# Modulation sums moved from GpSimd and ScalarE to VectorE, norm roots applied behind the products, and a reordered start

## The reference, cut to what matters

```python
for l in range(2):
    h = rms_norm(x, attn_norm[l])
    if l == 0: x = x + diff_attention(h, ...)           # 8 heads
    else:
        kw, vw = shared_kv(x, cos, sin, kv_norm, w_kv, k_norm)
        x = x + swa_sink_attention(h, ..., kw, vw)
    x = x + swiglu(rms_norm(x, ffn_norm[l]), w_gate_up[l], w_down[l])   # (silu(g) * u) @ w_down
```

```python
m = silu(cond) @ w_mod + b_mod      # cond: c and c_ctx; w_mod: 1024 x 6144, for two layers
h = rmsnorm(x, norm) * (1 + scale) + shift
```

## Time and profile before

| | |
|---|---|
| median of 3 runs | 3081.02 us (3073.94 to 3084.14) |
| profiled execution | 3078.21 us |
| its span, first to last instruction | 3076.3 us |
| mean granted TensorE clock | 0.953 |
| busy: TensorE, VectorE, ScalarE, GpSimd | 2794.8, 1682.3, 1269.5, 639.8 us (PE, DVE, ACT, POOL in the rows) |

### The profile page before, as it was taken

The page is one execution under the profiler, slowest core; times in us unless marked ns, Lnnn a source line. Parts: engine busy times, 40 slices in busy tenths (PEclk is TensorE's granted clock), DMA queues, the critical chain, the costliest instruction groups (busy, mean ns, idle before and its releaser), DMA issues.

```text
span 3076.3 us, 41620 instructions
## 1 busy us (share of the span) xinstructions
PE 2794.8 (91%) x14244; PEld 2339.8 (76%) x14244; DVE 1682.3 (55%) x2544; ACT 1269.5 (41%) x2121; POOL 639.8 (21%) x298
## 2 busy tenths in 40 slices
PE   4989899998687899997987899999997899899998
PEld 4777687886576778886875788888886887688886
DVE  5776534445665443435996465254455455464645
ACT  3444365654366365654211233132233466352422
POOL 0111077874011087873000000000000000000000
PEclk9999899998799999998997899999998999999999
DMA  3111244543100245443110111122111000222221
GB/s 122 42 44 60 82 157 158 177 157 117 42 19 25 82 171 175 163 162 103 55 52 31 55 55 61 56 69 69 61 36 55 28 29 8 69 89 89 96 94 63
DMA packets 67905, 252.07 MB, mean 82 GB/s; under 512 B 7456, under 2 KB 8736, under 8 KB 64928
## 3 DMA queue, kind: packets, MB, share of 16 engines
q1 hardware_dynamic: 67744, 249.99, 23.8%
HBM read 247.87 MB, written 2.10 MB: 81 GB/s over the span
## 4 chain that ended last, share of the span: by engine, by line
PE 45%; issue 21%; DVE 19%; POOL 7%; ACT 5%; DVEq 2%; ACTq 1%; DMA 0%; POOLq 0%
PE psum L1680 11%; PE psum L1681 11%; PE psum L1679 11%; POOL mod_p L485 7%; DVE work L1203 4%; DVE w_lo L1079 2%; PE psum L2035 2%; DVE work L1308 1%; ACT work L870 1%; ACT w_hi L568 1%; PE psum L1818 1%; DVE hx_lo L1302 1%; ACT sw_pt L882 1%; PE psum L1689 1%; PE psum L1796 1%
## 5 line engine op out<-in xcount | busy, mean ns | idle before, releaser
L1079 DVE TENSOR_TENSOR w_lo<-w_raw,w_hi 128x1024 fp32r<-128x1024 f32 (+3 forms) x334 | 447.8, 1341 | 415.8 <-ACT w_hi L568 403.5
L1679 PE MATMUL psum<-hx_hi,w_hi 128*128 128x512 f32 x1568 | 623.6, 398 | 29.6 <-DVE w_lo L1079 14.3
L1680 PE MATMUL psum<-hx_lo,w_hi 128*128 128x512 f32 x1568 | 625.1, 399 | 0.0
L1681 PE MATMUL psum<-hx_hi,w_lo 128*128 128x512 f32 x1568 | 623.7, 398 | 0.0
L485 POOL TENSOR_TENSOR mod_p<-mod_w,mod_c 128x1024 f32<-128x1024 f32 x192 | 547.6, 2882 | 186.7 <-ACT mod_p L553 150.8
L568 ACT ACTIVATE w_hi<-w_raw 128x1024 fp32r<-128x1024 f32 (+3 forms) x334 | 356.3, 1067 | 271.3 <-PE psum L1681 214.9
L475 POOL TENSOR_TENSOR tok_r<-tok_ms,half 128x4 f32<-128x4 f32 (+1 forms) x70 | 71.8, 1026 | 1857.7 <-DVE tok_ms L1003 1245.2
L1679 PEld LDWEIGHTS psum<-hx_hi,w_hi 128*128 128x128 f32 x1568 | 297.0, 189 | 80.6 <-issue 16.6
L1681 PEld LDWEIGHTS psum<-hx_hi,w_lo 128*128 128x128 f32 x1568 | 296.9, 189 | 70.4
L1680 PEld LDWEIGHTS psum<-hx_lo,w_hi 128*128 128x128 f32 x1568 | 297.6, 190 | 48.8
L1679 PE MATMUL psum<-a_hi,w_hi 128*128 128x512 f32 (+1 forms) x656 | 233.9, 357 | 19.4 <-DVE a_lo L1144 10.6
(11 more groups left out here) (263 smaller groups left out, 4954.4 us busy)
## 6 DMA issues: line engine op xcount, KB each, us to landing
mod_w<-in_w_mod SPq DMA_DIRECT2D x96, 512.0 KB, 3.6
w_raw<-in_fup SPq DMA_DIRECT2D x88, 512.0 KB, 4.6
w_raw<-in_cup SPq DMA_DIRECT2D x88, 512.0 KB, 3.5
w_raw<-in_fdown SPq DMA_DIRECT2D x32, 512.0 KB, 4.6
w_raw<-in_cdown SPq DMA_DIRECT2D x32, 512.0 KB, 3.5
w_raw<-in_da_qkv SPq DMA_DIRECT2D x8, 1536.0 KB, 6.4
w_raw<-in_fdown SPq DMA_DIRECT2D x16, 384.0 KB, 4.6
w_raw<-in_cdown SPq DMA_DIRECT2D x16, 384.0 KB, 3.0
```

Of the source, the lines that this page charges most:

```text
L1079: dve.tensor_tensor(w_lo[:, off:off + n], w_raw[:, raw:raw + n], w_hi[:, off:off + n].bitcast(F32), ALU.subtract).then_inc(s_lo, 1)
L1679: pe.matmul(dst, wh, xh, start=first, stop=False)
L1680: pe.matmul(dst, wh, xl, start=False, stop=False)
L1681: return pe.matmul(dst, wl, xh, start=False, stop=last)
```

## The change

- **Modulation.** VectorE alone does it: `scalar_tensor_tensor` multiplies a tile with a conditioning vector and sums it, with an accumulator output (`mods`), two instructions a tile. There are four slots for tiles; up stages take three tiles per group of four blocks, down stages four, the last down stage none. `load_mod` waits for `s_modd`, which VectorE raises after a tile. GpSimd's `modulation` and ScalarE's are gone.
- **Roots behind the products** (`late=True`), for the norms of the first block. What goes into the product is x times gain (`feed`: high part by ScalarE and low part by VectorE, made as each block of the stage before is evacuated), or x alone with the gain put into the weights (`wgain`, in 8 pieces of 256 columns, for keys, values and queries, so that the second scaling goes). TensorE sums the squares after 6 of 8 k-steps of the first pair and spreads the roots after it. In the feed-forward ScalarE copies the spread roots to `root_b`; VectorE multiplies the gate by them before the Silu (a new PSUM evacuation) and once more after it, on behalf of the value. In attention the root is the `scale` of the evacuation on ScalarE.
- **Start.** x and the first head's weights come in 8 slices each, behind positions, row constants and one gain; the second head's weights follow. Each slice is split, multiplied for all four token tiles (four PSUM banks) and squared as it comes. GpSimd computes the rotary angles and head tables, ScalarE the sines after slice 5. TensorE also makes the second head's first two projections ahead of the slots.

The diff's core (the plan, the start on VectorE and TensorE, the modulation, the feed-forward's evacuation, the fed input, and SyncE's loads):

```diff
-    norm(gain="attn_norm0", toks=SEQ)
+    norm(toks=SEQ, late=True)
     add("heads", 8, w="da_qkv")
-    add("resid", KT_D, k=KT_D, toks=SEQ, w="da_wo", src="O", gates=None, squares=SEQ, ready=7)
-    norm(gain="ffn_norm0", toks=SEQ)
-    ffn("ffn", 0, SEQ, "f", SEQ)
-    norm(gain="kv_norm", toks=SEQ)
-    add("kv", 2, w="sw_kv", tag="a", ctx=False)
-    norm(gain="attn_norm1", toks=SEQ, again=True)
-    add("q", 4, w="sw_q", tag="a", ctx=False)
+    add("resid", KT_D, k=KT_D, toks=SEQ, w="da_wo", src="O", gates=None, squares=SEQ, ready=7, feed="ffn_norm0")
+    norm(toks=SEQ, late=True, spread=True)
+    ffn("ffn", 0, SEQ, "f", SEQ, feed="none")
+    norm(toks=SEQ, late=True)
+    add("kv", 2, w="sw_kv", tag="a", ctx=False, wgain="kv_norm")
+    add("q", 4, w="sw_q", tag="a", ctx=False, wgain="attn_norm1")
...
+                dve.wait_ge(s_modl[s], 16 * i + 16 * (m["loads0"][s] + 1 + LOADS_MOD[s] * m["layer"]))
+                for c in range(2):
+                    r = dve.scalar_tensor_tensor(mod_out[c], mod_w[s].rearrange("p (a n) -> p a n", a=4), 1.0,
+                                                 mod_c[:, c, :].rearrange("p (a n) -> p a n", a=4), ALU.mult, ALU.mult,
+                                                 accum_out=mods[:, m["layer"], c, bass.ds(m["per"] * i + (m["n0"] + s), 1)])
+                r.then_inc(s_modd, 1)
...
                 def f(b, s, i):
+                    q = 2 * i + s // 2
+                    gate = wk[:, s // 2, 0:toks]
                     if s % 2 == 0:
+                        dve.wait_ge(s_mm, b + (st["block0"] + 1))
+                        dve.wait_ge(s_rbs, st["layer"] + 1)
+                        dve.tensor_tensor(gate, ps_of(st, s, 0, toks), root_b[:], ALU.mult).then_inc(s_ev, 1)
+                        dve.drain()
+                        dve.memset(ratio[:, 3:4], 0.0).then_inc(s_gsc, 1)
                         return
-                    q = 2 * i + s // 2
+                    dve.wait_ge(s_gate, q + (st["gate0"] + 1))
+                    dve.scalar_tensor_tensor(gate, gate, 1.0, root_b[:], ALU.mult, ALU.mult)
+                    dve.drain()
                     dve.wait_ge(s_mm, b + (st["block0"] + 1))
-                    dve.wait_ge(s_gate, q + (st["gate0"] + 1))
-                    dve.tensor_tensor(wk[:, 2 + s // 2, 0:toks], ps_of(st, s, 0, toks), wk[:, s // 2, 0:toks],
-                                      ALU.mult).then_inc(s_ev, 2)
+                    dve.tensor_tensor(wk[:, 2 + s // 2, 0:toks], ps_of(st, s, 0, toks), gate, ALU.mult).then_inc(s_ev, 1)
...
+                def feed(b):
+                    dve.wait_ge(s_hhi, st["feed0"] + b + 1)
+                    hi = hx_hi[:, b, :].bitcast(F32)
+                    if st["feed"] == "none":
+                        r = dve.tensor_tensor(hx_lo[:, b, :], X[:, b, 0:SEQ], hi, ALU.subtract)
+                    else:
+                        r = dve.scalar_tensor_tensor(hx_lo[:, b, :], X[:, b, 0:SEQ], vcol(st["feed"], b), hi,
+                                                     ALU.mult, ALU.subtract)
+                    r.then_inc(s_h, 1)
+                    add_square(b, b)
...
+            for k in range(KT_D):          # VectorE, start
+                dve.wait_ge(s_hhi, k + 1)
+                dve.scalar_tensor_tensor(hx_lo[:, k, :], X[:, k, 0:SEQ], vcol("attn_norm0", k), hx_hi[:, k, :].bitcast(F32),
+                                         ALU.mult, ALU.subtract).then_inc(s_h, 1)
...
+                dve.tensor_tensor(w_lo[:, cols], w_raw[:, cols], w_hi[:, cols].bitcast(F32), ALU.subtract)\
...
+                if k >= 2:
+                    add_first(k - 1)
...
             def linear(st):                # TensorE
-                pair(st, st.get("ready", 0), st["k"])
+                if st["src"] == "H" and st.get("late"):
+                    pair(st, 0, 6)
+                    sum_squares(st["late"])
+                    pair(st, 6, 8)
+                    spread_roots(st["late"])
+                else:
+                    pair(st, st.get("ready", 0), st["k"])
...
+                before = m["before"][slot] if isinstance(g, int) and g == 0 else m["n0"] + m["per"] * (g - 1) + slot
+                if before is not None:
+                    sp.wait_ge(s_modd, before + (MOD_TILES * m["layer"] + 1))
+                sp.dma_start(mod_w[slot], dram["w_mod"][...]).then_inc(s_modl[slot], 16)
```

More of the change, by code:

```diff
@@ L59, in make_plan @@
     stages = []
-    n = dict(block=0, lin=0, tile=0, gate=0, conv=0, norm=0, hset=0, rms=0)
+    n = dict(block=0, lin=0, tile=0, gate=0, conv=0, norm=0, hset=0, rms=0, ht=0)
     loads = [0, 0, 0, 0]
@@ L274, in program @@
         s_cact = sem("c_act_ready")
[L275 to L277 removed]
+        s_modl = [sem(f"mod_loaded{u}") for u in range(4)]
+        s_modd = sem("mod_summed")
         s_trig = sem("trig_args_ready")
@@ L288, in program @@
                     "krms", "krope", "klo", "rms", "rope", "qlo", "mx", "sinkx", "inv", "vzero", "invw", "osb", "olo", "kpr", "pr", "whi")
-        s_swt = {t: {k: sem(f"sw{t}_{k}") for k in sw_names} for t in ("a", "b")}
-        LOADS_IN = 6
+        only_a = ("krms", "kpr", "rms", "pr")
+        s_swt = {t: {k: sem(f"sw{t}_{k}") for k in sw_names if t == "a" or k not in only_a}
+                 for t in ("a", "b")}
+        LOADS_IN = 4
+        SQ_SLOT = (0, 1, 3)
+        LOADS_MOD = [sum(-(-(st["mod"]["count"] - u) // st["mod"]["per"]) for st in stages
+                         if st.get("mod") and st["mod"]["layer"] == 0 and u < st["mod"]["per"]) for u in range(4)]
         MOD_TILES = 48
@@ L488, in _ @@
+            angles()
+            head_gains()
+            head_table(0)
+            head_table(1)
             for st in stages:
-                if st.get("mod") and st["mod"][1] == 0:
-                    modulation(st["mod"][0])
-                if st["kind"] == "norm" and not st.get("again"):
+                if st["kind"] == "norm":
                     root(0, st["toks"] // P, s_ms, st["rms0"] + 1, s_pw)
@@ L951, in _ @@
                 if k == "norm":
-                    if not st.get("final"):
+                    if not st.get("final") and not st.get("late"):
                         norm(st)
@@ new lines, in _ @@
+            add_first(KT_D - 1)
+            means(stages[0])
+            for part in range(3):
+                if part < 2:
+                    dve.wait_ge(s_whi0, KT_D + part)
+                else:
+                    dve.wait_ge(s_hi, 2)
+                cols = slice(3 * D + D * part, 4 * D + D * part)
+                r = dve.tensor_tensor(w_lo[:, cols], second_raw[:, D * part:D * part + D], w_hi[:, cols].bitcast(F32),
+                                      ALU.subtract)
+            r.then_inc(s_lo, 1)
@@ L1281, in norm @@
                 toks = st["toks"]
-                if not st.get("again") and st is not stages[0]:
+                if st is not stages[0]:
                     means(st)
+                if st.get("late"):
+                    return
                 dve.wait_ge(s_rb, st["norm0"] + 1)
@@ L1859, in slot @@
                         turn_outputs(h - 1)
-                    if more:
+                    if more and not (first and i < 2):
                         project(j + 4, i, 1 - par, h + 1)
@@ L1932, in kv @@
                         .then_inc(S["kpj"], 1)
+                    if n == 0 and st.get("late"):
+                        sum_squares(st["late"])
                     if 2 <= n <= nt:
@@ L2081, in _ @@
                 if k == "norm":
-                    norm(st)
+                    if not st.get("late"):
+                        norm(st)
                     hset[0] += 0 if st.get("final") else 1
```

511 lines of the change are left out of this document (330 added, 181 removed).

## The result

| | before | after |
|---|---|---|
| median | 3080.27 us (3073.94 to 3084.14, 4 runs) | 3045.84 us (3041.13 to 3051.27, 4 runs) |
| ratio, 95% interval | | 0.9895 (0.9876 to 0.9913) |
| span profiled | 3076.3 us | 3044.8 us |
| mean granted TensorE clock | 0.953 | 0.955 |
| busy: TensorE, VectorE, ScalarE, GpSimd | in the table of before | 2791.2, 1888.6, 1083.0, 117.7 us |

What follows compares the result with a forecast made beforehand. TensorE, 91% busy, was taken to bound the kernel, with the time to win at the seams. -29 - 20 - 17 - 13 - 6 + 5 = -80 us gave 3000 us, range 2978 to 3045.

Steps and rivals of the forecast that it cites:

- Part 6: Feed-forward modulation moved to VectorE: +5 us, its loop group at 23.9 us against TensorE's 22.4.
- three weight blocks and four PSUM banks: Work ahead at a feed-forward stage's start, claimed as about 3 us of slack against VectorE's lateness.
- Rival B: Modulation loops: VectorE's gaps cost 0.34 us, not 0.16; 26 us a group, 42 in all, 3040 us; chance 0.16.
- Rival A: Modulation's product-and-sum with accumulator at half rate, 2.37 us an instruction; slower, 3178 us; chance 0.11.
- Rival D: No stall from the modulation and the two early projections pay: 2985 us; chance 0.13.
- Part 2: Two feed-forward norms: TensorE's idle and cold matmuls there go, -10 us each, -20; bounds 8 and 12.
- Part 5: End of layer 1, last down stage without modulation: last evacuation earlier, -6 us; bounds 0 and 8.
- evacuations 6.2 apart: Reading of layer 1's last down stage before: evacuations 6.2 us apart, where VectorE without modulation needs about 4.1 a step.
- Part 1: Start, x and first weights used slice by slice: score loop near 40.5 us, -29 us; bounds -20 and -34.
- rival C: Seams give less: late angles, DMA at keys, tails, or early start lost in the heads; 3020 us; chance 0.15.
- Part 3: Keys and values: first key rope at 773 instead of 790 us, -17 us; bounds 9 and 18.
- Part 4: Queries: second norm goes, first query rope at 820 instead of 833.1 us, -13 us; bounds 10 and 16.

Runs made afterwards that it cites:

- e2: Changed kernel with the modulation's loads still in SyncE's queue, but each issued three weight loads later: 3023.5 us.
- e10: Changed kernel with only the modulation tiles' loads issued from GpSimd's queue, the conditioning vectors' load on SyncE: 3021.5 us.
- e6: Changed kernel without the second scaling of the gate by the root, loads in SyncE's queue as they were: 3027.1 us.
- e7: e2's kernel, with VectorE's second and third tile in each up stage's last group put behind the fourth block's evacuation: 3019.6 us.
- e3: Changed kernel with each product-and-sum of a modulation tile on 16 elements a partition instead of 1024, loads and waits kept: 3014.6 us.
- e4: Kernel before, with only the modulation moved to VectorE alone; start, norms, keys and queries as before: 3078.0 us, ratio 1.0001.
- e8: Changed kernel with the last key's high and low part made ahead of the split of the queries' second weights: 3038.8 us.
- e5: Changed kernel with the modulation as before (GpSimd's products, ScalarE's sums), so start, norms, keys and queries alone: 3189.5 us.

## Why the prediction was right or wrong, point by point

**Part 6, the step that failed: +5 forecast, +34 measured.** The instructions were priced a little high (1.22 for 1.29). The wrong step is "a modulation load now waits for VectorE's tile and holds the next weight load, which lands 4.6 us later and is wanted two steps (11 us) on; it fits". The load is wanted one step on. From the end of the tile, load (4.8 us at 395.99) and ScalarE's split (1.1) take 6.7 us, and VectorE has one block of 4.9 us to do meanwhile, so it waits 1.7. My 23.9 us for VectorE's loop group was itself too long: freed of the waits it takes 22.6 (e2), almost TensorE's 22.4. So the group had nothing left to take up the wait, and each wait makes VectorE later for good. Freeing the loads gives 23 of the 34 us back (e2, e10), shortening the group instead 21 (e6). So the +5 had a part that was priced too high and left out the one that costs most. The 11 us that e2 still loses are a backlog that falls due at the step to the down stage: e7 takes 8 of them away. There my slack of "three weight blocks and four PSUM banks" did not help, since the next product needs a weights' low part that VectorE makes behind a modulation tile.

**Rival B** named the place, the size (42 forecast, 34 measured) and the mark (under 255 matmuls), but not the cause, so its nearness is luck: gaps in the loops stayed between 0.16 and 0.34, VectorE was busy 44 of 60 us, and with free loads its group takes 22.6 us and not 26. **Rival A** is refuted by the 1.22 us. The rule of the Trainium skill (Vector Engine (DVE) Microarchitecture Reference, "Points that are easy to get wrong") that this form halves throughput does not hold for these fp32 inputs: 1024 elements take 1225 ns with the accumulator, and the subtraction without it takes 1225 too. **Rival D** is refuted: e3 shows that even without any stall the seams give 64, to 3015.

**Part 2** was right: -10.1 and -11.1 for -10 each. **Part 5** was right: -7.6 for -6; e4 keeps a modulation in that stage and gains nothing there (shift -1.9 before it, -1.7 behind), so it is the stage's freedom from tiles that pays. The reading "evacuations 6.2 apart" holds only for the first group, which has the tiles; the last four gaps are 4.1 us, TensorE's own pace. The delay of the first group is what stayed to the end.

**Part 1**, -22.5 for -29. The slices end at 27.7, not 25 (1.5 us of it VectorE waiting behind the sines), the second weights' low part costs 4.1 for 3.7, and the first rope is at 33.3 for 31. The scores start at 45.3 for 40.5. The third rope ends at 42.3, but TensorE is in the second head's early projections until 44.0, and transposes and a copy follow; I had booked 1.1 us for all of it. Another 2 us go in the heads, as rival C had it. TensorE's clock in the first slots was low:

```profile
50.00:65.00 15.00, 12.68 (x34) 7.76 (x33) 9.94 (x27) 6.56 (x17) 2.01 (x2) 0.50 0.00 0
```

that is 1.2 GHz, after TensorE had been busy only 1.8 of 5 us from 45 to 50; before, the first slots from 70 to 85 ran at 1.00. Whether the clock or the waits of these slots cost the 2 us was not tried.

**Part 3**, -11.9 for -17. The first key rope comes 27.3 us behind the last down product (731.96 + 0.23 to 759.51), 25 forecast and 41.8 before. The wide split of 3.25 us stands ahead of the last evacuations, so the mean comes at 743.1, 10.9 behind the product instead of 8.7. Then 2.8 us go between the first rope and the last product: 14 of the keys' steps start 0.64 us or so after the one before, at half clock, where 4 did before; the others take 0.35.

**Part 4**, -7.5 for -13 to the first scores; the query rope comes 40.0 us behind the key rope, 30 forecast, 43.0 before. Here the failing step is the count from ScalarE's second split to the rope, 6.6 us: it left out the query's own product (5 us at half clock) and evacuation between them, 13.8 measured. And the norm that went was replaced by another wait, the last key's low part queued behind a split that the first query does not need. e8 takes it away: the query rope then comes 32.9 us behind the key rope, and the part brings 12.8 us. The 13 is thus what the seam can give, but with an order that the change did not have.

**The second attention**, where I had booked nothing, loses 4.6 us. 3.2 of them come between its units, and the traces of e2, e3 and e7 show the same 3.2; the cause stays open. The other 1.4 come behind the last scores, and e4, which has the code of before there, loses them too, so the change need not be their cause.

Counted together, the matched traces gain 31.5 us of the 80. Of the missing 48, 29 are part 6, 17 are parts 1, 3 and 4, which brought some 70% of their price together, and 5 are the second attention; parts 2 and 5 brought 3 more than forecast.

## What to carry to other kernels

When a wait is put into an in-order DMA queue, follow the transfer behind it to the step that consumes it, in steps of the slowest engine, and ask whether the engine that releases the wait is itself fed by that transfer: if so, add the wait to that engine's own work and compare the sum with the slowest engine's pace, instead of looking at each for itself. Place the wait where it is already satisfied, behind the loads that it could hold; the order of loads alone was worth 22 us here. An engine that is just under the pace of TensorE in a loop pays at the next stage whose first product needs its last result, so put its free work behind that result.

## What was unexpected in the hardware

- An fp32 product-and-sum of 128 x 1024 with accumulator output takes 1.22 us on VectorE, and reading the accumulator 0.08 us (ScalarE's takes 0.185).
- In e5 VectorE's gate scaling with both inputs in SBUF lasts until GpSimd's running product is done: 2.65 us for 0.69, 44 times of 44, each ending 0.55 us behind that product, while the form with one input in PSUM keeps 0.69 inside GpSimd's products, 22 times of 22. The Trainium skill (SBUF — State Buffer, "SBUF: two separate sides") describes such an exclusive lock on a shared port, held for a whole instruction; the trace agrees in the one form, while the subtraction of 1024, two SBUF inputs as well, is only stretched from 1.2 to 1.5 us, 84 times. Why the two forms differ is not shown.
- Loads issued by GpSimd cost nothing here beside a busy VectorE: 3021.5 us (e10) for 3023.5 with SyncE (e2), and 10.8 us lost for 10.9.
- GpSimd's small fp32 instructions on 128 x 128 take 0.3 to 0.9 us each, with gaps of about 0.16, as the profile has them; the 23 of the angles end at 20.6 us.
